# Three places in the order of work: the makers and place of the last two weight units, a split in the scan moved two half tiles on, and the mixer norm's factor products put together

## The reference, cut to what matters

```python
def first_block(...):                       # h: 272 x 1024
    u = rms_norm(h, mix_pre_g)
    hq, hf, hi, hg, cq, ckv, kpe, gates = split(u @ w_in)
    y_a = hgrn2_mixer(hq, hf, hi, hg, lb, hg_norm_g) @ w_hg_o
    y_b = mla_mixer(cq, ckv, kpe, q_a_norm_g, w_q_b, kv_a_norm_g, w_kv_b, cos, sin) @ w_mla_o
    gate_a, gate_b = split(sigmoid(gates + b_gate))
    h = h + rms_norm((gate_a * y_a + gate_b * y_b) @ w_out, mix_post_g)
    gt, up = split(rms_norm(h, ffn_pre_g) @ w_ffn_in)
    return h + rms_norm((silu(gt) * up) @ w_ffn_out, ffn_post_g)

def hgrn2_mixer(q, f_pre, i, g, lb, norm_g):      # 8 heads of 128, a gated linear recurrence
    fgate = lb + (1.0 - lb) * sigmoid(f_pre)
    o = hgrn2_chunk_scan(silu(q), 1.0 - fgate, i, log(fgate))
    return rms_norm(o, norm_g) * silu(g)          # the norm over each head's 128 channels

def mla_mixer(c_q, c_kv, ...):                    # starts with two norms over 256 channels each
    q = rms_norm(c_q, q_norm_g) @ w_q_b
    kv = rms_norm(c_kv, kv_norm_g) @ w_kv_b
    ...                                           # causal attention, 8 heads
```

```python
def conv_ffn(x, w_gate, conv_w, conv_b, w_up, w_down):
    a = causal_depthwise_conv(x @ w_gate, conv_w) + conv_b
    return (gelu(a) * (x @ w_up)) @ w_down
```

## Time and profile before

| | |
|---|---|
| time, median of 3 runs | 927.81 us (926.04 to 928.13) |
| profiled execution, its own time | 925.93 us |
| its span | 924.1 us |
| granted clock of TensorE, mean | 0.997 |
| PE (TensorE, matmuls) | busy 902.4 us, 98% of the span, x6767 |
| PEld (TensorE, weight loads) | 800.5 us, 87% |
| DVE (VectorE) | 678.8 us, 73% |
| ACT (ScalarE) | 465.2 us, 50% |
| POOL (GpSimd) | 223.1 us, 24% |
| data read | 151.28 MB, 165 GB/s over the span |

### The profile page before, as it was taken

One profiled execution on the slowest core, in us unless ns is written; L12 is line 12 of the kernel. 1 busy time (PEld: TensorE's weight loads), 2 busy tenths in 40 slices (PEclk: granted clock), 3 DMA queues, 4 the chain that ended last, 5 costly groups with the idle time before them and its releaser, 6 DMA issues.

```text
span 924.1 us, 16815 instructions
## 1 busy us (share of the span) xinstructions
PE 902.4 (98%) x6767; PEld 800.5 (87%) x6767; DVE 678.8 (73%) x1274; ACT 465.2 (50%) x936; POOL 223.1 (24%) x120
## 2 busy tenths in 40 slices
PE   9999999999999999999999999999999999999996
PEld 8879999889999888888888799887988888888885
DVE  5924986658655888767576768868888888788885
ACT  6334336564443574434444647776634445544343
POOL 3433421441213211642314342231100211210121
PEclk9999999999999999999999999999999999999999
DMA  8454444233433645655545354324445555455521
GB/s 296 150 205 143 176 141 139 84 122 138 137 105 130 227 175 207 226 184 194 197 162 222 136 191 157 106 87 163 179 157 208 183 188 209 155 223 183 214 105 46
DMA packets 23181, 153.67 MB, mean 166 GB/s; under 512 B 2864, under 2 KB 3248, under 8 KB 5568
## 3 DMA queue, kind: packets, MB, share of 16 engines
q1 hardware_dynamic: 22384, 150.43, 45.6%
q0 software_dynamic: 576, 2.10, 0.6%
q10 hardware_dynamic: 144, 0.07, 0.0%
HBM read 151.28 MB, written 1.05 MB: 165 GB/s over the span
## 4 chain that ended last, share of the span: by engine, by line
PE 60%; DVE 26%; ACT 10%; issue 4%; DVEq 0%; ACTq 0%
PE pb L506 58%; DVE wl L515 11%; ACT wh L512 4%; DVE FA L515 4%; DVE FA L518 4%; DVE FA L521 3%; ACT FA L512 3%; PE pb L509 2%; DVE wh L530 1%; ACT R L512 1%; DVE X L521 1%; DVE R L521 1%; DVE st L518 0%; DVE post L518 0%; DVE FA L524 0%
## 5 line engine op out<-in xcount | busy, mean ns | idle before, releaser
L506 PE MATMUL pb<-R,wh 128*128 128x256 f32 (+2 forms) x2224 | 550.4, 326 | 5.9 <-ACT R L512 2.0
L506 PE MATMUL pb<-R,wl 128*128 128x256 f32 (+1 forms) x1512 | 422.7, 281 | 0.0
L506 PEld LDWEIGHTS pb<-R,wh 128*128 128x128 f32 x2224 | 372.2, 189 | 45.4 <-ACT R L512 3.5
L515 POOL TENSOR_TENSOR wl<-raw,wh 128x1024 fp32r<-128x1024 f32 (+1 forms) x80 | 195.7, 2450 | 632.8 <-ACT wh L512 522.7
L515 DVE TENSOR_TENSOR wl<-raw,wh 128x1024 fp32r<-128x1024 f32 (+1 forms) x198 | 262.0, 1345 | 82.1 <-ACT wh L512 80.5
L506 PEld LDWEIGHTS pb<-R,wl 128*128 128x128 f32 x1512 | 284.3, 188 | 2.0 <-issue 0.3
L512 ACT ACTIVATE wh<-raw 128x1024 fp32r<-128x1024 f32 (+1 forms) x219 | 222.8, 1044 | 52.8 <-PE pb L506 50.8
L506 PE MATMUL pb<-wh,R 128*128 128x512 f32 (+2 forms) x724 | 234.4, 388 | 4.1 <-DVE R L515 2.1
L506 PEld LDWEIGHTS pb<-wh,R 128*128 128x128 f32 (+1 forms) x724 | 134.4, 186 | 36.7 <-ACT R L512 4.0
L512 ACT ACTIVATE FA<-pb 128x256 f32<-128x256 f32 (+7 forms) x240 | 94.0, 414 | 125.9 <-PE pb L506 111.0
L506 PE MATMUL pb<-wl,R 128*128 128x512 f32 (+2 forms) x372 | 143.3, 385 | 0.0
(11 more groups left out here) (122 smaller groups left out, 474.4 us busy)
## 6 DMA issues: line engine op xcount, KB each, us to landing
raw<-in_w SPq DMA_DIRECT2D x137, 1024.0 KB, 4.8
X<-in_x SPq DMA_DIRECT2D x2, 512.0 KB, 4.3
raw<-in_w SPq DMA_DIRECT2D x2, 512.0 KB, 6.5
post<-in_ffn_post SPq DMA_DIRECT2D x2, 512.0 KB, 4.6
post<-in_w POOLq DMA_DIRECT2D x2, 512.0 KB, 5.0
FA<-in_w POOLq DMA_DIRECT2D x2, 512.0 KB, 7.9
out<-X SPq DMA_DIRECT2D x4, 256.0 KB, 2.0
cst<-in_cst SPq DMA_DIRECT2D x1, 821.5 KB, 12.4
```

Source lines behind the costliest of these rows:

```text
L506: return self.real.matmul(*a, **k) if self.real else self
L515: return self.real.tensor_tensor(*a, **k) if self.real else self
```

## The change

It has three parts, and each changes only the order or the maker of work; what is computed stays as it was.

- **The end.** In MADE the letters of units 274 and 275 go from `p` to `d`, so VectorE makes their low parts instead of GpSimd. In ffn, for the last but one hidden tile of the second block (tile 30), the last step of the up tile's slot, the split of unit 275, is put ahead of `hidden` 30 instead of behind it.
- **The scan.** The split of unit 43 leaves the slot of gate 2's second half and is put two half tiles on, into the slot of gate 3's second half, behind its evac and ahead of the split of unit 44. What stood behind it in the list (level 6's decays, k_turn, the copies and the norm of ck) stands before it now.
- **The mixer norm's factors.** `o_scale` loses its cast (ScalarE) and its subtraction (VectorE); these become steps of their own, `o_part`. The four `o_scale` stand together behind qn 2, where before they stood ahead of the second kv group, behind its first unit, and later, one by one; the `o_part` come beside gates 9 to 12.

```diff
--- before.py
+++ after.py
@@ -276,7 +276,10 @@
 
     metas = [("meta", j) for j in range(4)] + [("meta_turn", g) for g in range(2)] + [("meta_state", g) for g in range(2)]
     lats = [[("lat", w, i) for i in range(3)] for w in ("ck", "cq")]
-    segs.append(("scan", p.take(), [metas, scan(0), scan(1), *lats, read(0) + read(1)]))
+    main = p.take()
+    at = [x[0] for x in main].index(("gemm", "gate", 2, 4, 8))
+    main[at + 2].insert(-1, main[at].pop())
+    segs.append(("scan", main, [metas, scan(0), scan(1), *lats, read(0) + read(1)]))
 
     for n in range(8):
         p.tile("kn", n)
@@ -293,7 +296,7 @@
     for n in range(8):
         p.tile("ya", n, True)
     heads = [[("m_score", h), ("m_exp", h), ("m_turn", h), ("m_value", h)] for h in range(8)]
-    segs.append(("latent", p.take(), [[("o_norm",)] + [("o_scale", h) for h in range(0, 8, 2)]] + heads))
+    segs.append(("latent", p.take(), [[("o_norm",)] + [(x, h) for x in ("o_scale", "o_part") for h in range(0, 8, 2)]] + heads))
 
     def ffn(name, gate, up, x, nt, down, order, before):
 
@@ -314,6 +317,8 @@
             p.slot(("gemm", gate, i, 0, 8), [(WCOLS[gate](i)[0], 128 * k, WCOLS[gate](i)[1]) for k in range(8)])
             p.slot(("gemm", up, i, 0, 8), [(WCOLS[up](i)[0], 128 * k, WCOLS[up](i)[1]) for k in range(8)],
                    ("hidden", name, i))
+            if name == "ffn2" and i == nt - 2:
+                p.slots[-1].append(p.slots[-1].pop(1))
             if i >= LAG:
                 p.wide(("down", name, i - LAG), DOWN[name][0], i - LAG, [rng(128 * j) for j in range(8)])
         segs.append((None, p.take(), []))
@@ -411,11 +416,11 @@
 KORD2 = [2, 3, 4, 5, 6, 7, 0, 1]
 MADE = ("dpdpddpdqdpdqdpdpdddpddpvpvdppqpdddppddddpddvqpqpqpdpdvddpdddpqddvdpddppddpddpddpddvvdddqvddddpd"
         "ddvvvdvdppdpdppvvpdqpdpqvddpvpdvpdddvpdvpdvdddvqdddqqpddpdpvddvdddddddpvvvdppvpppdvvdddvpdqddddd"
-        "pvddvddddvdddvdpqpdddddddqddddddddddddddppddpddddddqddddvddvdvddddddpdvvdddvdvpdddpp")
+        "pvddvddddvdddvdpqpdddddddqddddddddddddddppddpddddddqddddvddvdvddddddpdvvdddvdvpddddd")
 MIX = {
     "scan": "..abc.aabc..bb.c..ab.bc...a.b.b..cc...bcb.c..a..cc...bc.b.ca.bbcd.c..cbcbad.bd.c.e.b.ecf.eff.ff."
             "ff.f",
-    "latent": "...a.......a..a...........a.b....b.fgf.b..e.f.g.e.dc.f.ba...c.ge.i.cg.ecdh.dh....i...i.h.d.ih",
+    "latent": "...a............aaaa.........b...a.b.afgf.b.a.e.af.g.e.dc.f.b...c.ge.i.cg.ecdh.dh....i...i.h.d.ih",
     "out1": "............c.cac..aacbab.a.aa..bb.bcbbcc.c...",
     "ffn1": "..aaa..aa..c....caac....bbc..b..b..b.b...b............",
     "maps": "...a.....acbabcbc..cc.bbb.ede.eed.ecag.agcdgcggadc.b.bfcgbefdc.ab.dgfbe.dbhffbab.hcfhcccf.ghiecb"
@@ -1395,7 +1400,7 @@
                 elif kind == "o_norm":
                     e.wait_ge(*dve.at("o_var"))
                     e.activation(r8, r8, ACT.Sqrt).then_inc(*act.up("o_sd"))
-                elif kind == "o_scale":
+                elif kind == "o_part":
                     h0, = a
                     e.wait_ge(*dve.at(("o_mul", h0)))
                     e.activation(OPERAND["oh"][:, h0:h0 + 2, 0, :], OT[:, h0:h0 + 2, :],
@@ -1798,6 +1803,9 @@
                     e.tensor_tensor(ov.rearrange("p h t -> p (h t)"), ov.rearrange("p h t -> p (h t)"), banks.of(step)[:, :],
                                     ALU.mult).then_inc(*dve.up(("o_mul", h0)))
                     banks.ended(step, dve.now())
+                elif kind == "o_part":
+                    h0, = a
+                    ov = OT[:, h0:h0 + 2, :]
                     e.wait_ge(*act.at(("oh", "h", h0)))
                     e.tensor_tensor(OPERAND["oh"][:, h0:h0 + 2, 1, :], ov, rf(OPERAND["oh"][:, h0:h0 + 2, 0, :]),
                                     ALU.subtract).then_inc(*dve.up(("oh", "l", h0), ("oh", "l", h0 + 1)))
```

## The result

The changed kernel takes 929.08 us (median of 22 runs, 927.23 to 931.26), the kernel before 927.37 us in 22 runs beside it. The ratio is 1.0021, 95% interval 1.0014 to 1.0028: slower by 1.95 us (1.3 to 2.6). The forecast was 0.9 us faster, called no change. The number lies inside the range, and that is luck: the sign of one of the three terms was wrong, the lower clock was left out of another, and the third was worth more than forecast, which hid part of the rest.

The account below looks back on a forecast made before the run. TensorE, busy 98% of the span, was taken as the bound, so only its waits count: -1.6 - 1.5 + 2.2 = -0.9 us, median 927.81 to 926.9, called no change; range 924.2 to 929.3.

Parts of the forecast that it names:

- its own signs of being wrong: No wait over 1 us between 160 and 175, granted clock falling near 170, or a new wait between 205 and 260.
- Term C: Mixer norm's factors: wait at 203.60 goes, four o_scale in a row cost less; -1.5 us, bounds 0 and -1.7.
- Term A: The end: TENSOR_SCALARs freed from GpSimd, last wait 2.08 to 0.5; -1.6 us, bounds -1.3 and -2.1.
- The replay: Scan, step by step from rows and order: VectorE waits, reciprocal 2.2 late, TensorE waits 3.0 for CQ's squares; +2.2 us.
- Term B: Scan's split: 0.9 gained at k_turn, then TensorE waits 3.0 for CQ's squares; +2.2 us, bounds -0.9 and +2.4.
- the new wait costs half the clock too: Rival, 25%: scan's 3.0 wait drops the clock, at most 1.7 us; sum +0.8, 928.6.
- its restart: At 203.60, some 0.15 us gained beyond the wait of 0.71, which is counted from a matmul's modelled end.
- a change of kind: In term C, four o_scale in a row pay it once: 3 x 0.2 = 0.6 us less on TensorE.
- gates 8 to 12: Where o_part casts and subtractions come back, 4 x 0.6 on each engine; TensorE had no wait there before.
- term C is given back: Rival, 10%: o_parts delay exp and weights of gates 9 to 13, TensorE waits there; sum +0.6, 928.4.

Follow-up runs that it names:

- the filled kernel: The whole change plus seven further matmuls on constants in the scan's wait of 2.9 us; ratio 1.0002, against 1.0021 for the change.
- both waits cured: Kernel before with only the factors part, fourth o_scale between qpe 2 and qpe 3, banks of tm2 and tm1 fixed to 2 and 3; ratio 0.9983.
- the kernels with and without the cover: Factors part alone on the kernel before, banks fixed: fourth o_scale between qpe 2 and qpe 3, ratio 0.9983; all four behind qn 2, 0.9999.
- one letter: Kernel before with unit 43 in MADE from d to v, at its old place, so VectorE makes its high part too; ratio 0.9988.
- the same seven in the shorter wait at the end: Kernel before plus seven matmuls of 256 columns on constants in front of the tail's product with hidden tile 31; ratio 0.9995.

## Why the prediction was wrong, step by step

The prediction named its own signs of being wrong, and two of the three came: the granted clock fell near 170, and a new wait stands at 214.81. Three steps failed. The lower clock was left out of the scan's term. Term C counted a gain that wasn't there and two waits too few. And the last wait was priced without its lower clock.

**Term A, -1.6.** Right in mechanism and in the size of the wait: -1.67 in the change, -1.42 alone, and the two TENSOR_SCALARs take 0.41 where they took 2.04 and 1.86. The trace agrees with what the Trainium skill says of the shared port (Advanced Engine Details and Errata, section VectorE Performance Modes): with GpSimd's two subtractions gone, only these operations got shorter, and the TENSOR_TENSOR at 904.22, beside the same subtraction, had taken its 0.42 before. The worth was undersized. The prediction took from the earlier trace rows that the clock stays up behind the last wait. That row was one execution, and seven of the eight profiles with such a wait show the fall, worth 1.3 to 1.6 us. So the end alone measured -2.4.

**Term B, +2.2.** The replay was right to 0.1 us: low part at 161.59 (forecast 161.6), reciprocal 164.59 (164.6), wait 2.90 at 169.46 (3.0 near 169.5), lag +2.1 to +2.2 in every profile where the clock stayed up. The value of 1.28 for the table load, kept from the row, held: it starts at 158.84 after the change, and the tanh behind it at 160.13 (forecast 160.17). What failed is the weighing: "the new wait costs half the clock too" was given 25% and left out of the sum, on the ground that the 2.08 us wait had not cost it. The fall came, for 3.4 us and 1.68 us of time (forecast: 3.4 and 1.7 at most), and the filled kernel shows that it counts in the median. The ground was one execution, and an exception among them. The Trainium skill (TensorE: Matmul & The Clock Gate, section HAM oscillation) says that waits between bursts of matmuls throttle the clock again. The runs agree with that, for shorter waits than those of its example, which has 3 to 5 us: here 2.1 to 3.0 us and less were enough in many executions.

**Term C, -1.5.** The largest error: measured -0.11 in the section and +0.95 at 545, together +0.84. The forecast was made of the wait at 203.60 with its restart, 0.86, and of 0.6 for a change of kind that four products in a row pay once. The wait went, as forecast. The 0.6 wasn't there. TensorE's timeline after has the four in a row and the matmuls behind them:

```profile
204.81 3.61 PE L511 MATMUL pb<-FA,cst 128*128 128x256 f32 x16
208.07 0.59 PE L511 MATMUL pb<-R,wh 128*128 128x256 f32 x2
```

They hold TensorE for 3.26 us from start to start (forecast: about 2.7), and before, standing apart, the one at 195.16 held it for 0.67 and the one at 209.46 for 0.80: four times that is 2.7 to 3.2, so nothing was saved. With both waits cured the factors gave -0.98, which is the 0.86 and 0.1 more. Then the prediction checked gates 8 to 12, where the o_part went, but not the place that the third o_scale left. There the product itself was the cover: take it away and the wait it hid comes out, 0.63, a lag of 0.85 between the kernels with and without the cover. And the change of the order turned the rotation of banks, for another 0.95 us at a tile 330 us away. The order of before and after shows it, on one row, as one semaphore more. The steps from the forecast of -1.5 to the measured +0.84 are +0.5, +0.85 and +0.95. The rival "term C is given back" was right that the section would give nothing (-0.11), by the wrong mechanism: no new wait of TensorE over 0.6 us stands at gates 9 to 13.

**The sum.** By what the parts showed: scan +2.1 and the clock +1.7, factors -0.1 and the bank +0.95, end -1.5 and its clock -1.3 (an estimate: 1.5 in seven of eight): +1.85, measured +1.95. The forecast had the scan's wait and the end's wait right and missed 1.7, 2.3 and -1.3. The last hid a part of the first two.

**What stays open.** How often the clock falls behind a wait: three of five profiles in the scan, while the change's median fits nearly always. Why behind one and not the other, at the same length, isn't known either. The three that fell all contained the factors part, the two that did not lacked it, and nothing of that part stands before 190 us; five are too few to say, and the times of the scan alone (+3.4 against a lag of +2.1) speak for falls without it. Which part of the forecast 0.6 for the change of kind was misread wasn't taken apart. And it wasn't tried why the last wait grows (2.08 to 2.66) when TensorE comes earlier.

## What to carry to other kernels

A step that one engine waits for should not be moved in front of one that is due, however much room it has at its old place: either take the engine that is idle there to make it (here one letter, 1 us), or leave it. Before an instruction is moved away, ask what it covered where it stood, not only what it will cost where it goes. And after a change of order, compare the waits of the busiest engine over the whole program: buffers that are handed out in rotation carry a change to places far from it.

## What the runs showed of the hardware

A wait of TensorE of 2.1 to 3.0 us was followed by some 3.4 us at the lower clock often and not always: behind 10 of the 13 such waits in these profiles, at 1.3 to 1.7 us each. Behind the waits of 1.04 us and less at the end it was not. But the length of one wait doesn't decide it: behind two of 0.9 and 0.7 us near 328 and 330 us, which all 17 profiles have, the clock fell in 6, at 0.7 to 0.9 us each. Behind the wait of 1.46 near 645 us it fell in 8 of 17, but there the next wait for ScalarE, at 651, is so much shorter (0.36 in before, against 1.5 to 1.6 where the clock stays up) that it costs nothing. So a single profile can be 0.7 to 1.7 us off the median at each such place, which is as much as a whole term here. Filling the scan's wait with useless matmuls cost nothing (lag +2.09 with, +2.14 without) and gave 1.8 us back; the same seven in the shorter wait at the end overran it and still cost nothing in the median.
